# Constant products on TensorE around six norms of a two-block transformer kernel

## What is computed

```python
def rmsnorm(x, g):
    xf = x.astype(jnp.float32)
    y = xf * lax.rsqrt(jnp.mean(xf * xf, axis=-1, keepdims=True) + EPS)
    return (y * g.astype(jnp.float32)).astype(x.dtype)

# end of the first block
    h3 = rmsnorm(x, g_ple[i])
    gate = jax.nn.sigmoid(jnp.einsum("bsd,de->bse", h3, w_ple_gate[i]))
    x = x + gate * jnp.einsum("bsk,kd->bsd", p[i], w_ple[i])
return rmsnorm(x, g_final)

# second block, two layers
    h = rms_norm(x, pre_mix_norm[layer])
    mix = gated_deltanet_mixer(...)                 # layer 0
    k_sh, v_sh, c_sh = shared_kv(x, kv_norm, ...)   # layer 1
    mix = forgetting_attention_mixer(...)           # layer 1
    x = x + rms_norm(mix, post_mix_norm[layer])
    f = swiglu(rms_norm(x, pre_ffn_norm[layer]), w_ffn_in[layer], w_ffn_out[layer])
    x = x + rms_norm(f, post_ffn_norm[layer])
```

## Time and profile before

| What | Value |
|---|---|
| Median of 3 runs | 2693.11 us (2691.86 to 2693.34) |
| Profiled execution, its own time | 2696.52 us |
| Its span | 2694.7 us |
| TensorE products, busy | 2411.8 us (89%), 11758 instructions |
| TensorE weight loads, busy | 1905.5 us (71%) |
| VectorE, ScalarE, GpSimd busy | 1150.2, 826.7, 487.1 us |
| Mean granted TensorE clock | 0.94 |

### The profile page before, as it was taken

One profiled execution on the slowest core, in us unless ns is written; L12 is line 12 of the kernel. 1 busy time (PEld: TensorE's weight loads), 2 busy tenths in 40 slices (PEclk: granted clock), 3 DMA queues, 4 the chain that ended last, 5 costly groups with the idle time before them and its releaser, 6 DMA issues. The chain is left out here.

```text
span 2694.7 us, 30222 instructions
## 1 busy us (share of the span) xinstructions
PE 2411.8 (89%) x11758; PEld 1905.5 (71%) x11758; DVE 1150.2 (43%) x1594; ACT 826.7 (31%) x1152; POOL 487.1 (18%) x177
## 2 busy tenths in 40 slices
PE   6987998999998869978998789999786987899997
PEld 5874667788786658838886668888675656688886
DVE  2026653442534467545555354442321373544423
ACT  4211662331222344332222232221221372322212
POOL 3431003100000334414452310000042303000000
PEclk9988999999999879989989889999888898899998
DMA  3210002222221212200000122222123101222221
GB/s 130 93 53 30 1 33 78 78 97 96 89 94 63 86 49 93 95 29 9 0 0 0 62 79 94 94 94 94 63 79 127 60 1 63 79 94 94 96 101 53
DMA packets 28811, 183.51 MB, mean 68 GB/s; under 512 B 3472, under 2 KB 3600, under 8 KB 7712
## 3 DMA queue, kind: packets, MB, share of 16 engines
q1 hardware_dynamic: 28704, 182.05, 18.8%
HBM read 179.91 MB, written 2.13 MB: 68 GB/s over the span
## 5 line engine op out<-in xcount | busy, mean ns | idle before, releaser
L223 POOL TENSOR_TENSOR weights_low<-weights_raw,weights_high 128x2048 fp32r<-128x2048 f32 (+1 forms) x67 | 305.9, 4566 | 1031.1 <-ACT weights_high L206 630.3
L206 ACT CAST weights_high<-weights_raw 128x2048 fp32r<-128x2048 f32 x164 | 311.1, 1897 | 488.3 <-PE psum L397 475.9
L233 DVE TENSOR_TENSOR weights_low<-weights_raw,weights_high 128x2048 fp32r<-128x2048 f32 x97 | 222.4, 2293 | 364.0 <-ACT weights_high L206 364.0
L395 PE MATMUL psum<-ffn_split,weights_high 128*128 128x512 f32 x704 | 280.8, 399 | 2.0 <-DVE ffn_split L1328 2.0
L397 PE MATMUL psum<-ffn_split,weights_low 128*128 128x512 f32 x704 | 280.7, 399 | 0.0
L396 PE MATMUL psum<-ffn_split,weights_high 128*128 128x512 f32 x704 | 278.6, 396 | 0.0
L395 PE MATMUL psum<-block_split,weights_high 128*128 128x512 f32 (+1 forms) x608 | 246.1, 405 | 15.6 <-POOL block_split L545 5.9
L397 PE MATMUL psum<-block_split,weights_low 128*128 128x512 f32 (+1 forms) x608 | 244.7, 402 | 0.0
L396 PE MATMUL psum<-block_split,weights_high 128*128 128x512 f32 (+1 forms) x608 | 243.4, 400 | 0.0
L395 PEld LDWEIGHTS psum<-ffn_split,weights_high 128*128 128x128 f32 x704 | 133.3, 189 | 33.3 <-issue 2.1
L396 PEld LDWEIGHTS psum<-ffn_split,weights_high 128*128 128x128 f32 x704 | 133.4, 189 | 33.1
(11 more groups left out here) (431 smaller groups left out, 4305.9 us busy)
## 6 DMA issues: line engine op xcount, KB each, us to landing
weights_raw<-in_weights SPq DMA_DIRECT2D x162, 1024.0 KB, 4.7
fox_minus_c<-minus_c_rows SPq DMA_DIRECT2D x16, 256.0 KB, 5.7
x_stream<-in_x SPq DMA_DIRECT2D x2, 1024.0 KB, 8.0
out<-x_stream SPq DMA_DIRECT2D x8, 256.0 KB, 2.1
rope_table<-rope_tables SPq DMA_DIRECT2D x1, 1024.0 KB, 5.4
weights_raw<-in_weights SPq DMA_DIRECT2D x1, 768.0 KB, 4.1
weights_raw<-in_weights SPq DMA_DIRECT2D x1, 512.0 KB, 3.5
ple_in_p_tiles<-in_p SPq DMA_DIRECT2D x1, 512.0 KB, 3.7
```

Of the source, the lines that this page charges most:

```text
L206: self.nc.scalar.copy(self.high[:, chunk.slot, 0:width], self.raw[:, chunk.slot, 0:width]).then_inc(self.high_ready, 1)
L223: self.nc.gpsimd.tensor_tensor(out=self.low[:, chunk.slot, 0:width], in0=self.raw[:, chunk.slot, 0:width], in1=self.high[:, chunk.slot, 0: ...
L233: self.nc.vector.tensor_tensor(out=self.low[:, n % 2, 0:width], in0=self.raw[:, n % 2, 0:width], in1=self.high[:, n % 2, 0:width].bitcast( ...
L395: nc.tensor.matmul(bank, wh, ah, start=first, stop=False)
```

## The change

A helper issues products of the identity with the first 128 columns of the constants into PSUM bank 5. Nobody reads the result, and no semaphore is attached. A norm takes a pair `idle`: the first number of such products stands on TensorE's queue between the sum over partitions and the wait for `rstd`, the second behind the spread. Six calls, in six stages, give a pair; the other norms keep (0, 0) and issue none. Nothing else changes.

```diff
+        def keep_busy(pe, bank, times):
+
+            for _ in range(times):
+                nc.tensor.matmul(psum[:, bank, 0:P], identity, const[:, 0:P], start=True, stop=True)
...
             def __init__(self, s, source, tiles, gain_at, split=None, plain=None, add_to=None, given=False,
-                         sum_next=False, prefix="norm"):
+                         sum_next=False, prefix="norm", idle=(0, 0)):
...
+                self.idle_bank, self.idle = 5, idle
...
                 last.then_inc(self.summed, 1)
+                keep_busy(pe, self.idle_bank, self.idle[0])
                 pe.wait_ge(self.rstd, 1)
...
                 last.then_inc(self.spread, 1)
+                keep_busy(pe, self.idle_bank, self.idle[1])
...
-            ple(norm_of(x, DT, lambda t: gain("g_ple", t), split=split, given=True), split, gates)
-            rms_normalize("norm_final", x, DT, lambda t: gain("g_final", t), plain=x, given=True, sum_next=True)
+            ple(norm_of(x, DT, lambda t: gain("g_ple", t), split=split, given=True, idle=(8, 12)), split, gates)
+            rms_normalize("norm_final", x, DT, lambda t: gain("g_final", t), plain=x, given=True, sum_next=True, idle=(8, 60))
...
+                    rms_normalize("norm_gdn_out", mix, DT, lambda t: gain("post_mix_norm_2", t), add_to=x, given=True, sum_next=True, idle=(8, 70))
...
+                    fox_kv(norm_of(x, DT, lambda t: gain("kv_norm_2", t), split=split, given=True, idle=(8, 12)), split, keys, values, f_raw)
...
+                linear("fox_q", 2, split, norm=norm_of(x, DT, lambda t: gain("pre_mix_norm_2", DT + t), split=split, given=True, idle=(8, 12)),
...
+                rms_normalize("norm_fox_out", queries, DT, lambda t: gain("post_mix_norm_2", DT + t), add_to=x, given=True, sum_next=True, idle=(8, 70))
```

More of the change, by code:

```diff
@@ L2535, in block_two @@
                     linear("gdn_out", 2, split, copy_to(mix), result=mix)
-                    rms_normalize("norm_gdn_out", mix, DT, lambda t: gain("post_mix_norm_2", t), add_to=x, given=True, sum_next=True)
+                    rms_normalize("norm_gdn_out", mix, DT, lambda t: gain("post_mix_norm_2", t), add_to=x, given=True, sum_next=True, idle=(8, 70))
             def feed_forward(layer):
@@ L2554, in block_two @@
                 with nc.sbuf_tensor("fox_f_raw", [FOX_HEADS, T], f32) as f_raw:
-                    fox_kv(norm_of(x, DT, lambda t: gain("kv_norm_2", t), split=split, given=True), split, keys, values, f_raw)
+                    fox_kv(norm_of(x, DT, lambda t: gain("kv_norm_2", t), split=split, given=True, idle=(8, 12)), split, keys, values, f_raw)
                     fox_rows(f_raw, minus_c, minus_c_in)
-                linear("fox_q", 2, split, norm=norm_of(x, DT, lambda t: gain("pre_mix_norm_2", DT + t), split=split, given=True),
+                linear("fox_q", 2, split, norm=norm_of(x, DT, lambda t: gain("pre_mix_norm_2", DT + t), split=split, given=True, idle=(8, 12)),
                         finish=copy_to(queries, FOX_HD ** -0.5))
@@ L2561, in block_two @@
                 linear("fox_out", 2, split, copy_to(queries), result=queries)
-                rms_normalize("norm_fox_out", queries, DT, lambda t: gain("post_mix_norm_2", DT + t), add_to=x, given=True, sum_next=True)
+                rms_normalize("norm_fox_out", queries, DT, lambda t: gain("post_mix_norm_2", DT + t), add_to=x, given=True, sum_next=True, idle=(8, 70))
             feed_forward(1)
```

## The result

The change makes the kernel slower: 2705.05 us as the median of 8 runs (2702.72 to 2712.02) against 2693.23 for 8 runs of the kernel before, a ratio of 1.0045 with a 95% interval of 1.0036 to 1.0055. That is +11.8 us; the forecast was +10.5. The profiled execution took 2704.87 us, its span is 2703.1.

What follows compares the result with a forecast made beforehand. Around the norms the path is a chain on VectorE, ScalarE and GpSimd, so a low clock costs only TensorE's own work there; delays and late filler ends less clock gains at nine sites summed to +10.5 us, 2703.5, range 2695 to 2711.

Steps and rivals of the forecast that it cites:

- The first batch: Eight products between sum and spread delay the spread: 2.1 us at the low clock, 0.85 us at the high (ple).
- fox_kv: Stage with a first batch at the low clock: +2.1 us for the late spread, 0.4 back, net +1.7 us.
- The second batch past the chain: Products behind the spread outlast VectorE's chain and close the stage: norm_final +5.5 us, norm_gdn_out and norm_fox_out +3.4 each.
- gdn_in: Stage without fillers finds the high clock: sum and spread gain 1.7 us, first bank loses 0.3, net -1.4 us.
- ffn0: L1298 at the high clock -0.8 us, plus half of 1.5 us on first products: -1.55 us.
- ffn1: Sum at the high clock -0.8 us, plus half of 2.9 us on fifteen first products: -2.3 us.
- three signs of being wrong: Spread not late, fillers ending before VectorE's last L469, or ffn0 and ffn1 gaining over 4 us each.
- The price of a pass: Each added product is two passes, 0.112 us each at the high clock, 0.212 low; slower fetching could add 4 us.
- Rival 1: Fillers half as dear if reloading the same identity were skipped: -5.8 us, 2687.3; 5%.
- Rival 4: Fillers never raise the clock, so the batches run slow without gains: about +60 us, 2753; 3%.
- everything gained: Rival: TensorE's busy time in nine low-clock stretches halves with fillers hidden: 26.9 us less, 2666.2; 3%.
- throttled time times lost share: Trainium skill's price for the 113.9 us of low-clock stretches, idle time counted as lost: an estimated 57 us gained.

Runs made afterwards that it cites:

- first_only: Only the eight products before the spread kept at all six places, second number 0, against the kernel before: 2705.65 us, 1.0041.
- second_only: Only the products behind the spread kept, first number 0 in all six pairs, against the kernel before: 2693.37 us, 1.0005.
- two_columns: The change with its added products two columns wide in place of 128, same places and number, against the kernel before: 2754.12 us, 1.0229.
- everywhere: tails_only plus 42, 61 or 12 products behind spreads and four in mlp and ffn stages, against the kernel before: 2682.38 us, 0.9952; again 2681.42 us.
- second_sized: No products before the spread, 36 behind it in norm_final, 55 in the result norms, none elsewhere, against the kernel before: 2694.26 us, 0.9990.
- everywhere_first8: The run everywhere with eight products put before the spread in its seven norms: 2697.45 us, 1.0010 to the kernel before.
- tails_only: No products in the norms, but in TensorE's pauses ahead of them (stage ends and fox_rows), against the kernel before: 2690.25 us, 0.9973.

## Why the prediction was right

**The first batch** was the right mechanism with about the right size. Directly, by VectorE's first L532 after the sum: it starts 1.73, 1.95, 2.50, 1.87 and 1.96 us later than before at norm_final, norm_gdn_out, fox_kv, fox_q and norm_fox_out, and 0.93 us later at ple. I had 2.1 and 0.85. In ple, fox_kv and fox_q the first banks gave back 0.31, 0.32 and 0.70 us of it, where I had at most 0.4, 0.4 and 0.8. Doubling the batch cost 1.7 to 2.0 us a place against 1.79 by the passes, and first_only is +11 us as expected, with the luck in its parts that is told above.

**The second batch past the chain**: norm_final's fillers end 3.39 us after VectorE by the rows above (3.4 forecast). The three stages came out at 5.12, 3.22 and 3.24 us for 5.5, 3.4 and 3.4; each a little under, since there the clock rose 3.7 to 4.1 us after the first filler, not 4.5 (at fox_kv it was 5.2). The terms of the two batches don't add at a site: first_only and second_only give 2.34 and 4.28 at norm_final for 5.12 together, as the delay of VectorE's chain hides behind the end of the second batch. The prediction had said that behind a filler end a later spread does not count in full.

**What was mis-sized.** gdn_in: -1.4 forecast, -0.12 measured. Its sum was fast (1.02 us), but the clock fell soon after, its spread took most of its old time (1.94 us) and more first products were slow; I had put only 0.3 us on that. ffn0: -1.55 forecast, -0.68. I had given the clock half a chance to last over the pause between the last filler and the first product. In the change and in second_only it was lost shortly before or after the first product of ffn0 and of ffn1, four times of four. But in the change it was back 5.5 us after the start of ffn1's sum, which before took 9.0 us, so that ffn1 still gained 2.06 for 2.3: the number is near, but not for the reason I had given. fox_kv came out 0.5 us dearer than forecast. The sites sum to 12.7 us for 10.5. The profiled span grew by less, 8.4, because stages that nobody touched, which I had taken as fixed, were shorter; the medians, 11.8, lie between. That the forecast is within 1.3 us of them is closer than its terms are, and in part luck. None of the three signs of being wrong came: the spread was late, the fillers of the three norm stages ended after VectorE's last L475, and ffn0 and ffn1 gained less than 4 us each.

**The price of a pass** held to the digit (120 in 13.56 us, 0.112 each), so no fetching of instructions made itself felt, and a reload of the same identity was never skipped (12326 loads for 12326 products). Rival 1, the fillers at half the price, is out by these rows. Rival 4, that the clock never rises, is what two_columns built on purpose: the forecast 2753 came out at 2754.12, so the prices of the sum hold from that side too. The 26.9 us of "everything gained" were not reached: the best kernels found gain 12 to 15 us. The estimate from the Trainium skill's rule of throttled time times lost share ("TensorE: Matmul & The Clock Gate", Terms), 57 us, is further off still, and the traces do not agree with the rule: by the mean clock in the profile of everywhere (0.964), an estimated 130 us fewer are spent at 1.2 GHz than before, and the gain was 12 to 13 us; in the change itself an estimated 70 us fewer went with a longer time. Its statement in Part 2, step 1, that products keep their order agrees with the traces here: in the change the spread starts 5.25 us after the sum's start instead of 2.54, behind sixteen filler passes, though the value it needs is there 2.8 us earlier.

## What to carry to other kernels

Work that only keeps an engine's clock up must stand where the engine waits and nothing behind it does: at the end of a stage, sized to end before the engine that closes it, or in a pause measured in the trace. The same product in front of a short chain's next link is paid as soon as it no longer fits into the pause there: three products fitted into 0.70 us, eight did not. Before pricing a low clock, count the busy time that the engine has on the path while the clock is low; idle time at a low clock cost nothing here. And check the clock at every site after such a change, as moving the work also moves the moments at which the clock falls.

## What the runs showed of the hardware

- After the same pause of 3.21 us TensorE's sum ran at 1.2 GHz in one execution and at 2.4 GHz in another (1.84 and 1.02 us). The length of the pause alone does not tell: the sum kept the high clock after 2.78 us (ffn0 in second_sized) and after 3.47 us (fox_kv in everywhere), and had lost it after 2.76 us (ffn1 in everywhere_first8) and 2.92 us (fox_kv in tails_only).
- Times of one kernel spread by several microseconds with or without fillers: second_only ranged from 2688.29 to 2701.66 us, the kernel before beside it from 2689.18 to 2697.11. That such pauses cause the spread is not shown.
- At the low clock an fp32 pass of 2 columns and one of 128 columns have the same 0.213 us between starts, and 120 passes of 2 columns ran for 25.6 us without the clock rising.
- With TensorE writing another PSUM bank for 9 to 13 us beside them, the chains of VectorE, ScalarE and GpSimd kept their length: the three norm stages of second_sized differ from before by at most 0.09 us.
